# Running the seam between the third output projection and the third MLP by two token halves

## What is computed

```python
m = _short_conv(h, w_in[i], conv_w[i // N_MIXERS], w_out[i])
hres = hres + _rmsnorm(m, norm_g[i, 1])
h = _rmsnorm(hres, norm_g[i, 2])
hres = hres + _rmsnorm(_sqrelu_mlp(h, w_up[i], w_down[i]), norm_g[i, 3])
```

## Time and profile before

| | us |
|---|---|
| median of 3 runs | 1973.28 |
| lowest and highest | 1971.84, 1976.45 |
| profiled execution, its own time | 1971.16 |
| span of its trace, first to last instruction | 1969.4 |
| busy in the span: PE, DVE, ACT, POOL | 1887.1, 1387.8, 839.2, 149.8 |
| mean granted clock of PE | 0.981 |

### The profile page before, as it was taken

How to read it: one execution, slowest core, us unless ns; L and a number is a source line. 1 busy time by engine, 2 the same in 40 slices (tenths; PEclk the granted TensorE clock), 3 DMA queues, 4 the chain that set the end, 5 groups by cost and what they waited for, 6 DMA issues and landing times.

```text
span 1969.4 us, 30367 instructions
## 1 busy us (share of the span) xinstructions
PE 1887.1 (96%) x12322; PEld 1699.5 (86%) x12322; DVE 1387.8 (70%) x2110; ACT 839.2 (43%) x1286; POOL 149.8 (8%) x126
## 2 busy tenths in 40 slices
PE   7999889999999899999998999999899989999996
PEld 6876777899999788989898999999899868988995
DVE  8676738788786866666649877776655469777764
ACT  4555434444443444444435444443422245444441
POOL 3000021000000320000012000000300130000001
PEclk9999999999999999999999999999899989999998
DMA  5220121232333221111111322222122212323221
GB/s 182 67 105 22 54 86 65 86 108 86 108 108 107 86 86 65 44 44 44 65 65 65 108 96 98 89 105 108 45 87 105 86 66 106 107 86 107 107 86 43
DMA packets 26085, 166.54 MB, mean 85 GB/s; under 512 B 3808, under 2 KB 4064, under 8 KB 6624
## 3 DMA queue, kind: packets, MB, share of 16 engines
q1 hardware_dynamic: 25232, 163.52, 23.6%
q10 hardware_dynamic: 720, 1.14, 0.2%
HBM read 162.55 MB, written 2.10 MB: 84 GB/s over the span
## 4 chain that ended last, share of the span: by engine, by line
PE 46%; DVE 4%; ACT 1%; issue 0%; ACTq 0%
PE ps L2857 6%; PE ps L2858 6%; PE ps L2859 6%; PE ps L2873 4%; PE ps L2872 4%; PE ps L2871 4%; PE ps L402 4%; PE ps L404 4%; PE ps L403 4%; DVE ps L560 1%; DVE h L577 1%; DVE z_lo L511 1%; PE ps L2644 0%; PE ps L2646 0%; PE ps L2645 0%; PE ps L449 0%
## 5 line engine op out<-in xcount | busy, mean ns | idle before, releaser
L402 PE MATMUL ps<-z_hi,w_hi 128*128 128x512 f32 (+1 forms) x736 | 259.8, 353 | 31.3 <-DVE z_lo L511 28.0
L384 DVE TENSOR_TENSOR w_lo<-w_raw,w_hi 128x2048 fp32r<-128x2048 f32 x93 | 214.0, 2301 | 64.6 <-ACT w_hi L373 64.5
L403 PE MATMUL ps<-z_lo,w_hi 128*128 128x512 f32 (+1 forms) x736 | 255.3, 347 | 0.0
L404 PE MATMUL ps<-z_hi,w_lo 128*128 128x512 f32 (+1 forms) x736 | 254.8, 346 | 0.0
L2857 PE MATMUL ps<-arena,w_hi 128*128 128x256 f32 (+2 forms) x768 | 245.5, 320 | 0.5 <-DVE acc L2134 0.5
L2858 PE MATMUL ps<-arena,w_hi 128*128 128x256 f32 (+2 forms) x768 | 245.9, 320 | 0.0
L2859 PE MATMUL ps<-arena,w_lo 128*128 128x256 f32 (+2 forms) x768 | 245.4, 320 | 0.0
L373 ACT ACTIVATE w_hi<-w_raw 128x2048 fp32r<-128x2048 f32 x93 | 177.1, 1905 | 71.8 <-PE ps L404 59.0
L402 PEld LDWEIGHTS ps<-z_hi,w_hi 128*128 128x128 f32 x736 | 142.9, 194 | 56.7 <-issue 22.7
L404 PEld LDWEIGHTS ps<-z_hi,w_lo 128*128 128x128 f32 x736 | 142.5, 194 | 17.5
L403 PEld LDWEIGHTS ps<-z_lo,w_hi 128*128 128x128 f32 x736 | 143.1, 194 | 16.8 <-issue 0.7
(11 more groups left out here) (415 smaller groups left out, 5081.8 us busy)
## 6 DMA issues: line engine op xcount, KB each, us to landing
w_raw<-wstream SPq DMA_DIRECT2D x151, 1024.0 KB, 4.8
out<-h SPq DMA_DIRECT2D x8, 256.0 KB, 2.0
w_raw<-wstream SPq DMA_DIRECT2D x2, 512.0 KB, 6.2
h<-xT ACTq DMA_DIRECT2D x4, 256.0 KB, 6.6
h<-xT SPq DMA_DIRECT2D x4, 256.0 KB, 6.1
rope_cs<-pT SPq DMA_DIRECT2D x1, 512.0 KB, 5.5
acc<-pos SPq DMA_DIRECT2D x1, 256.0 KB, 10.5
acc<-lam SPq DMA_DIRECT2D x1, 128.0 KB, 9.9
```

What stands on the lines that cost most here:

```text
L384: dve.tensor_tensor(w_lo[:, slot, :], w_raw[:, slot, :], w_hi[:, slot, :].bitcast(f32), ALU.subtract).then_inc(wlo, 1)
L402: pe.matmul(dst, wh, zh, start=(k == 0), stop=False)
L403: pe.matmul(dst, wh, zl, start=False, stop=False)
L404: last = pe.matmul(dst, wl, zh, start=False, stop=(k == nk - 1))
```

## The change

From the third output block on, the 512 tokens are handled as two halves of 256 (`part_of`), and the queues of all four engines are written anew up to the end of the second up block of the MLP. PE now runs eight half blocks (`turn_pe`): both last output blocks for the first half, both for the second, both first up blocks for the first half, both for the second. The statistics of a half, and the spreading of its root, stand inside the half blocks that follow. DVE, ACT and POOL do the work of the norms once for each half (`turn_dve`, `turn_act`, `turn_sums`), all with 256 columns. The product of L560 goes to `tmp` in SBUF instead of a PSUM bank. A weight slot of an output block is free one half block later than before, since both last output blocks are in use until the second half is through. The second half's semaphores are taken from names that earlier stages have done with (`RENEWED`).

```diff
+        def turn_square(act, pi, hf, k, pre=0):
+            a, e = in_h(pi, hf)
+            if k >= 2:
+                act.wait_ge(*ev("summed", pi, hf, k - 2, pre))
...
+            act.activation(sq[:, k % 2, a:e], src, ACT.Square).then_inc(ev("squared", pi, hf)[0], 1)
...
+        def turn_act(act, pi):
...
+            turn_square(act, pi, 1, 7)
+            turn_root(act, pi, 1)
+            turn_zhi(act, pi, 0, 5)
+            turn_square(act, pi, 0, 0, 1)
+            turn_square(act, pi, 0, 1, 1)
+            turn_zhi(act, pi, 0, 6)
+            act_next(act, g0 + 1)
+            turn_square(act, pi, 0, 2, 1)
+            turn_square(act, pi, 0, 3, 1)
+            turn_zhi(act, pi, 0, 7)
+            for k in range(4, 8):
+                turn_square(act, pi, 0, k, 1)
+            for k in range(8):
+                turn_zhi(act, pi, 1, k)
+                turn_square(act, pi, 1, k, 1)
+                if k == 3:
+                    turn_pre_root(act, pi, 0)
...
+        def turn_prod(pi, hf, k):
+            a, e = part_of(pi, hf)
+            return tt(4 + k % 2, e - a)
+        def turn_scale(dve, pi, hf, k):
...
+            dve.scalar_tensor_tensor(turn_prod(pi, hf, k), ac(k)[:, a:e], smc(POST[pi][0], POST[pi][1] + k), turn_roots(pi, hf),
+                                     op0=ALU.mult, op1=ALU.mult).then_inc(ev("scaled", pi, hf)[0], 1)
+        def turn_add(dve, pi, hf, k):
...
+            dve.tensor_tensor(h[:, k, a:e], h[:, k, a:e], turn_prod(pi, hf, k), ALU.add).then_inc(ev("resid", pi, hf)[0], 1)
...
+        def turn_dve(dve, pi, evict):
...
+            turn_scale(dve, pi, 0, 0)
+            add(0, 0)
+            lo(0, 0)
+            evict(1, 1 if late else 3)
+            add(0, 1)
+            dve_lo(dve, g0, g0 % 2)
+            lo(0, 1)
...
+            lo(0, 6)
+            add(0, 7)
+            dve_lo(dve, g0 + 1, (g0 + 1) % 2)
+            lo(0, 7)
+            turn_scale(dve, pi, 1, 0)
+            for k in range(8):
+                add(1, k)
+                lo(1, k)
+                if k == 5:
+                    turn_pre_rcp(dve, pi, 0)
...
+        def turn_pe(pe, pi, nk, z, ready):
+            turn_last_block(pe, pi, 0, 0, nk, z, ready, {})
+            turn_last_block(pe, pi, 1, 0, nk, z, ready, {})
+            turn_last_block(pe, pi, 0, 1, nk, z, ready, {5: lambda: turn_columns(pe, pi, 0), 11: lambda: turn_spread(pe, pi, 0)})
+            turn_last_block(pe, pi, 1, 1, nk, z, ready, {})
+            turn_first_block(pe, pi, 0, 0, {2: lambda: turn_columns(pe, pi, 1), 10: lambda: turn_spread(pe, pi, 1)})
+            turn_first_block(pe, pi, 1, 0, {8: lambda: turn_pre_stat(pe, pi, 0)})
+            turn_first_block(pe, pi, 0, 1, {})
+            turn_first_block(pe, pi, 1, 1, {4: lambda: turn_pre_stat(pe, pi, 1)})
...
-            pool_sum(pool, 9, S, META)
-            pool_sum(pool, 10, S, META)
+            turn_sums(pool, 4)
...
-            dve_post(dve, 4, S, META, nxt_c0=META, early=lambda: dve_lo(dve, B_MLP3 + 1, (B_MLP3 + 1) % 2))
...
+            turn_dve(dve, 4, evict_out)
...
-            pe_post_stat(pe, 4, S, META)
...
+            turn_pe(pe, 4, KD, lambda x, k: out_part(x, k)[:, 0:S], out_ready)
```

More of the change, by code:

```diff
@@ new lines, in turn_zhi, with turn_col @@
+        def turn_zhi(act, pi, hf, k):
+            zi, (a, e), (x, y) = NEXT_Z[pi], in_h(pi, hf), part_of(pi, hf)
+            act.wait_ge(*ev("resid", pi, hf, k))
+            if k == 0 and hf == 0:
+                act.wait_ge(ps_full, turn_base(pi) + 2 * turn_tiles(pi))
+            act.activation(z_hi[:, k, x:y], h[:, k, a:e], ACT.Copy, scale=smc(GAIN[zi][0], GAIN[zi][1] + k)).then_inc(ev("zhi", pi, hf)[0], 1)
+        def turn_col(pi, hf):
+            n = len(turn_starts(pi, hf))
+            return cols[:, R_COL + 2 * hf:R_COL + 2 * hf + n]
@@ new lines, in turn_columns @@
+        def turn_columns(pe, pi, hf):
+            a, e = in_h(pi, hf)
+            n, sums = len(turn_starts(pi, hf)), turn_sums_at(pi, hf)
+            pe.wait_ge(*ev("summed", pi, hf, 6))
+            for i, x in enumerate(turn_starts(pi, hf)):
+                pe.matmul(sums[:, i:i + 1], ssum[:, a + x:a + x + P], ones[:, 0:1], start=True, stop=True)
+            pe.wait_ge(*ev("squared", pi, hf, 7))
+            for i, x in enumerate(turn_starts(pi, hf)):
+                last = pe.matmul(sums[:, n + i:n + i + 1], sq[:, 1, a + x:a + x + P], ones[:, 0:1], start=True, stop=True)
+            last.then_inc(ev("stat", pi, hf)[0], 1)
@@ new lines, in turn_spread, with turn_pre_stat @@
+        def turn_spread(pe, pi, hf):
+            pe.wait_ge(*ev("rstd", pi, hf))
+            for i, x in enumerate(turn_starts(pi, hf)):
+                last = pe.matmul(turn_roots(pi, hf)[:, x:x + P], turn_col(pi, hf)[:, i:i + 1].to_broadcast([P, P]), ident[:, :],
+                                 start=True, stop=True)
+            last.then_inc(ev("spread", pi, hf)[0], 1)
+        def turn_pre_stat(pe, pi, hf):
+            c0 = turn_size(pi)[1]
+            pe.wait_ge(*ev("summed", pi, hf, 7, 1))
+            for a, e, dst in turn_spare(pi, hf):
+                last = pe.matmul(dst, ones[:, :], ssum[:, c0 + a:c0 + e], start=True, stop=True)
+            last.then_inc(ev("stat", pi, hf)[0], 1)
@@ new lines, in turn_last_block @@
+        def turn_last_block(pe, pi, f, hf, nk, z, ready, between):
+            b = turn_next(pi) - 2 + f
+            a, e = part_of(pi, hf)
+            nt, base = turn_tiles(pi), turn_base(pi)
+            for t in range(nt):
+                ready(f, hf, t)
+                before = nt * hf + t - 3
+                if before >= 0:
+                    pe.wait_ge(ps_free, base + 2 * nt * (before // nt) + nt * f + before % nt + 1)
+                dst = turn_tile(pi, f, hf, t)
+                for k in range(nk):
+                    if nk * t + k in between:
+                        between[nk * t + k]()
+                    w = (nk * t + k) * P
+                    wh, wl = w_hi[:, b % 2, w:w + P], w_lo[:, b % 2, w:w + P]
+                    zh, zl = z(0, k)[:, a:e], z(1, k)[:, a:e]
+                    pe.matmul(dst, wh, zh, start=(k == 0), stop=False)
+                    pe.matmul(dst, wh, zl, start=False, stop=False)
+                    last = pe.matmul(dst, wl, zh, start=False, stop=(k == nk - 1))
+                last.then_inc(ps_full, 1)
@@ new lines, in turn_first_block @@
+        def turn_first_block(pe, pi, g, hf, between):
+            b, ntok = turn_next(pi) + g, turn_size(pi)[0]
+            slot = pair_of(b) % 2
+            a, e = part_of(pi, hf)
+            if hf == 0:
+                pe.wait_ge(wlo, b + 1)
+                pe.wait_ge(ps_free, turn_base(pi) + turn_tiles(pi) * (3 + g))
+            for k in range(KD):
+                if g == 0:
+                    pe.wait_ge(*ev("zlo", pi, hf, k))
+                for o in range(2):
+                    if 2 * k + o in between:
+                        between[2 * k + o]()
+                    w = (o * KD + k) * P
+                    wh, wl = w_hi[:, b % 2, w:w + P], w_lo[:, b % 2, w:w + P]
+                    dst = banks(slot, o, ntok)[:, a:e]
+                    zh, zl = z_part(0, k)[:, a:e], z_part(1, k)[:, a:e]
+                    pe.matmul(dst, wh, zh, start=(k == 0), stop=False)
+                    pe.matmul(dst, wh, zl, start=False, stop=False)
+                    last = pe.matmul(dst, wl, zh, start=False, stop=(k == KD - 1))
+                    if hf and k == KD - 1:
+                        last.then_inc(ps_full, 1)
```

229 lines of the change are left out of this document (217 added, 12 removed).

## The result

| | kernel before | changed kernel |
|---|---|---|
| median of 10 runs | 1972.99 | 1979.76 |
| lowest and highest | 1970.24, 1976.45 | 1977.85, 1980.61 |
| profiled execution, its own time | 1971.16 | 1980.23 |
| span of its trace | 1969.4 | 1978.4 |

The change makes the kernel slower: the ratio is 1.0036, with a 95% interval from 1.0027 to 1.0044, or 5.3 to 8.7 us. A second measurement of the same code, beside other runs of the kernel before, gave 1.0050 (1.0036 to 1.0063, 5 runs); +6.5 to +7.5 us were expected of it and it came to +9.9, with an interval that overlaps the first. The forecast was 1979.5.

What follows compares the result with a forecast made beforehand. PE's and DVE's chains met at the first down block, with DVE to set it afterwards; its steps gave `t_first` at 1624.9, plus 22.7 made 1647.6, +6.2 us, so 1973.28 + 6.2 = 1979.5 us, range 1972.5 to 1984.0.

Steps and rivals of the forecast that it cites:

- The join, and DVE at it: At the first down block: DVE's last split sets the start, at 1647.6 against 1641.34; PE waits about 2 us.
- Step 1: Start of DVE's chain: the first scale comes at 1586.7, 11.8 us earlier than 1598.47.
- Steps 2 to 6: DVE from first scale to `t_first`: cycles, other work, waits, ACT's queue and collisions with POOL, 38.2 us.
- Step 2: DVE's sixteen cycles of 256 columns in place of eight: 1.15 or 1.38 us each, 20.2 us.
- Step 4: DVE's waits inside the stage, for `w_hi`, a `z_hi` behind the root and the last one: 3.7 us, bounds 0 and 5.
- Step 5: ACT's queue: the second half's first `z_hi` stands behind squares waiting for POOL, delaying DVE by about 2.2 us.
- Step 6: DVE operations with two SBUF operands wait for POOL's additions, in both halves: 4.5 us, bounds 0 and 12.
- `t_first` to the down block: DVE from `t_first` to the end of its last split: 22.7 us, against 24.8 before.
- no collision of the add: Rival: POOL's additions fall into gaps or cost little, so the join moves +2 to +4 us; chance 0.20.
- Faster: DVE hardly waits: Rival: ACT keeps ahead, nothing collides, all sixteen cycles run at 1.15 us; join at 1634.8, -6.5 us; chance 0.10.
- Read to the letter: DVE and POOL in the same stage: full exclusive lock without overlap, both directions, about +10 us instead of +6.2.

Runs made afterwards that it cites:

- e4: Changed kernel with 48 matmuls of 256 columns more on PE, into a free PSUM bank: ratio to before 1.0033, stage 75.96 us.
- e10: Changed kernel with both reciprocals of the norm ahead of the MLP doing 64 of 256 columns: ratio to before 1.0026, stage 73.69 us.
- e10b: Kernel before with the reciprocal of the norm ahead of the third MLP doing 128 of 512 columns: ratio 0.9997, stage 68.65 us.
- e1: Changed kernel with the product of scale in a free PSUM bank again: ratio to before 1.0019, stage 71.92 us.
- e6: Changed kernel with ACT's queue reordered, first-half squares 4 to 7 alternating with the second half's first z_hi: ratio to before 1.0033, stage 74.12 us.
- e7: Changed kernel with ACT's order of e6 and the product in PSUM of e1: ratio to before 1.0020, stage 71.01 us.
- e8: Changed kernel with the same instructions in another order on DVE and ACT, product still in SBUF: ratio to before 0.9988, stage 67.35 us.
- e2: Changed kernel with POOL adding only 8 of 256 columns of each square for the norm ahead of the MLP: ratio to before 1.0013, stage 70.52 us.
- e9: Kernel of e8 with the product of scale in a free PSUM bank too: ratio to before 0.9986, stage 66.93 us.
- e3: Kernel before with the product of scale in SBUF instead of PSUM, in pieces of 512 columns: ratio 1.0029, stage 75.77 us.
- e11: Kernel of e9 with the fourth sum of token halves and the weight sums put behind the down block's splits: ratio to before 1.0001, stage 64.68 us.

## Why the prediction was right

The forecast for the profiled execution was +6.2 us; it was +9.1: 0.4 ahead of the stage, 7.7 in it and 0.9 behind it, rounded. On the medians it was +6.8, and the profiled execution of the second measurement gives +7.3 (7.2 in the stage, -0.3 behind it). So the mechanism and the order of the terms held, but that 1979.5 lies 0.3 from the measured median is in part luck: the sum is 1 to 1.5 us short in the stage. By its own steps:

- **The join, and DVE at it.** Right, in place and mechanism (2.09 us of wait at the first down matmul; e4, e10, e10b). PE's spare time was real. The wait at the join doesn't measure how late DVE is, though: the third up block has to wait for DVE's evictions as well (`L407 <- DVE tmp` above, 0.9 us; 2.2 us in e1, where the wait at the join is 0.5).
- **Step 1, the start.** 14.2 us from the last `w_lo` to the first scale were forecast (1586.7 - 1572.51), 14.55 measured. 0.4 short.
- **Steps 2 to 6, first scale to `t_first`.** Forecast 38.2 us, measured 39.2, and 38.6 in the second trace. In it:
  - Step 2: pieces of 0.47, 0.42 and 0.48 us, against 0.49, 0.42 and 0.48. Yet what the other terms leave over for the 16 cycles is 21.1 us, where 20.2 were taken. The second half's 1.38 for a cycle fits (1.40 in e1), so the 0.9 missing lie mostly in the first half, where two low parts also wait 0.18 and 0.19 for `z_hi`.
  - Step 4, waits: 0.72 and 0.98 for `w_hi`, 0.76 behind the root, 0.58 at the last: 3.0, 0.7 under what was taken. The first trace has 0.67 more for the columns of the second half, a wait that the prediction doesn't have and the second trace doesn't, either.
  - Step 5: 1.98 us of gap, of which 0.2 stand in every cycle, so 1.8; 2.2 forecast. As a saving it is worth less than its size, as e6 and e7 show: when the gap goes, additions of POOL meet other work.
  - Step 6: a little undersized. It took 0.52 us in six cycles and 1.4 in the first half, 4.5 in all. Measured are about 0.55 in each of six cycles, 3.3, and 1.7 in the first half (two adds, and the low parts behind both `w_lo`, 0.96 and 0.95 in place of 0.48): 5.0. The additions took 0.73 to 0.74, as forecast, though the working given for it (1.33 less half of what isn't fixed, with 0.2 fixed) comes to 0.77.
- **`t_first` to the down block.** 22.7 forecast, 22.8 measured; L2533 took 1.76 in place of 2.31, which is the 0.5 that was expected.
- **Not in the forecast: the clock behind the join.** In the first trace PE ran at half clock from 1650.3 on, 0.42 us from matmul to matmul (rows above) in place of 0.23. The first stretch behind the join in the changed kernel, and in the kernel before:

```profile
1649.45:1660.00 10.55, 10.55 (x39) 8.48 (x40) 9.94 (x12) 4.29 (x7) 0.00 (x0) 0.84 0.24 91
```

```profile
1641.34:1652.00 10.66, 10.66 (x46) 8.41 (x46) 10.66 (x12) 6.10 (x8) 0.00 (x0) 1.00 0.25 96
```

The granted clock is 0.84 against 1.00. The fall came after the 2.09 us of waiting, but it belongs to the execution and not to the change: the second trace of the same code, with a wait of 2.10 us at the same place, has 1.00, and 327.7 us behind the join in place of 328.9. So the fall goes with 1.2 us, some 5 matmuls (39 against 44). e8, with 2.10 us, and e4, with 2.09, have 1.00 too; e2, with 2.09, has 0.84. The second trace, then e8:

```profile
1648.95:1659.45 10.50, 10.49 (x44) 8.27 (x45) 10.50 (x12) 4.30 (x7) 0.00 (x0) 1.00 0.23 92
```

```profile
1643.08:1653.60 10.52, 10.52 (x44) 8.27 (x45) 10.52 (x12) 4.29 (x6) 0.00 (x0) 1.00 0.25 93
```

The rivals: "no collision of the add" (+2 to +4) is what e1 made of it, +3.1 in the stage. "Faster: DVE hardly waits" (-6.5) is the nearest to e8 and e9, which reach -1.5 and -1.9 in the stage. Its condition (steps 4, 5 and 6 below 4 us together) and its price don't go together: -6.5 takes all three at nothing, and with 4 us left it would be -2.5. In e8 the first scale is 0.35 us later than it took, the way to `t_first` 29.1 us in place of 26.0, since low parts and adds still meet POOL (0.52 for a low part, 0.50 for an add) and PE's second spread holds DVE for 0.65 us, and from there to the down block it is 23.7 in place of 22.1, since both first operations of `t_first` meet POOL (1.76 and 1.98 us, where 1.23 and 1.14 are their own time in e2).

The Trainium skill (SBUF — State Buffer, section "SBUF: two separate sides") says that a DVE operation with two SBUF inputs and a GpSimd operation take an exclusive lock. The traces agree that either blocks the other: POOL holds DVE's adds (e1, e2 and e3 against their counterparts), and a `w_lo` held POOL's addition at 1605.49 (six additions took 7.13 us there, last line below). Read to the letter it gave +10 us; the rows show an overlap of 0.13 to 0.15 us at the end (an add of 0.42 ended 0.29 after POOL, one of 0.69 in e3 0.54 after), and the stage came out at +7.7 and +7.2, nearer to the rows. That alone doesn't decide between the two, since other terms were off by as much as 0.9; the measured overlap does.

```profile
1605.49 7.13 POOL L653 TENSOR_TENSOR ssum<-ssum,sq 128x256 f32<-128x256 f32 x6 [2.13 <-ACT sq L555]
```

## What to carry to other kernels

Splitting a stage in two lets the matrix engine start early, but if another engine is on time only to the microsecond at the next join, count that engine's chain: its work, its waits in the new order, and what its operands now share with a third engine. Where an intermediate result lies can matter more than the split: adds that read SBUF and PSUM and now read SBUF twice cost 4 to 7 us here. And take a wait out by ordering the queue so that each result has one other piece of work ahead of its use; work put off behind a join came back in e11, where the engine is full. Before a part of a single trace is explained, a second trace of the same code is worth having: here 1.8 us of the +9.1 were missing from it.

## What was not expected of the hardware

An operation with one tensor in SBUF and a column of scalars (L2548, `acc<-h,sm`, 256 columns, four of them) took 1.97 us in all beside additions of POOL (e6, and the same in e7, e8 and e9) and 1.14 without them. The prediction had counted only operations with two tensors in SBUF as held up. And the place in which a collision happens is not chance: in the changed kernel (six of the second half's eight cycles) and in e3 (the last six of its eight adds) the queues fall into step, so that the same add meets the same addition cycle after cycle, at nearly its full length.
